# Work moved around and into a gated scan: TensorE's order in the mixer of a two-block network

## What is computed

```
def step(S, inp):
    qc, kc, gc, vc = inp
    b = jnp.cumsum(gc, axis=2)
    diff = b[:, :, :, None, :] - b[:, :, None, :, :]
    decay = jnp.exp(jnp.where(mask, diff, -jnp.inf))
    scores = jnp.einsum("bhtk,bhsk,bhtsk->bhts", qc, kc, decay)
    o = (jnp.einsum("bhts,bhsv->bhtv", scores, vc)
         + jnp.einsum("bhtk,bhkv->bhtv", qc * jnp.exp(b), S))
    b_end = b[:, :, -1, :]
    S = (jnp.exp(b_end)[..., None] * S
         + jnp.einsum("bhsk,bhsv->bhkv", kc * jnp.exp(b_end[:, :, None, :] - b), vc))
    return S, o
...
o = _rmsnorm(o, g_o.reshape(HGRN_HEADS, HGRN_V)).reshape(B, L, B_W).astype(h.dtype)
b_out = o * jax.nn.silu(og)
return jnp.concatenate([a_out, b_out], axis=-1) @ w_out, s_f, s_b
```

## Time and profile before

| | |
|---|---|
| median of 3 runs | 2659.68 us (2659.16 to 2661.69) |
| the profiled execution: its time, its span | 2657.78 us, 2656.0 us |
| mean granted TensorE clock | 0.992 of full |
| PE busy | 2580.4 us, 97% |
| DVE busy | 1200.5 us, 45% |
| ACT busy | 1111.1 us, 42% |
| POOL busy | 889.5 us, 33% |
| HBM | 141 GB/s over the span |

### The profile page before, as it was taken

The page is one execution under the profiler, slowest core; times in us unless marked ns, Lnnn a source line. Parts: engine busy times, 40 slices in busy tenths (PEclk is TensorE's granted clock), DMA queues, the critical chain, the costliest instruction groups (busy, mean ns, idle before and its releaser), DMA issues.

```text
span 2656.0 us, 43966 instructions
## 1 busy us (share of the span) xinstructions
PE 2580.4 (97%) x17121; PEld 2297.4 (86%) x17121; DVE 1200.5 (45%) x1801; ACT 1111.1 (42%) x1544; POOL 889.5 (33%) x1092
## 2 busy tenths in 40 slices
PE   7999999998999999999999999888999999999999
PEld 5777779988887777787777898888999999999999
DVE  4222225237652222252232257654456666556744
ACT  4322334535343222244122247536574554446543
POOL 1222222230022222222233226214554445552554
PEclk9999999999999999999999999999999999999999
DMA  7443542430024334423434434224554444553444
GB/s 278 143 177 139 158 163 98 141 111 1 32 101 162 136 141 152 143 97 142 143 143 143 143 135 151 88 91 152 182 188 163 140 153 181 185 180 112 159 182 151
DMA packets 58527, 376.89 MB, mean 142 GB/s; under 512 B 6223, under 2 KB 12007, under 8 KB 14216
## 3 DMA queue, kind: packets, MB, share of 16 engines
q1 hardware_dynamic: 56988, 371.53, 38.9%
q10 hardware_dynamic: 1388, 3.16, 0.8%
HBM read 370.46 MB, written 3.16 MB: 141 GB/s over the span
## 4 chain that ended last, share of the span: by engine, by line
issue 53%; PE 27%; POOL 17%; DVE 1%; POOLq 0%; DMA 0%; ACT 0%; SPq 0%; DVEq 0%; ACTq 0%
POOL WL L1932 17%; PE PSA L569 8%; PE PSA L570 8%; PE PSA L571 8%; PE PSA L1307 0%; PE PSA L651 0%; POOLq L397 0%; PE PSA L1205 0%; PE PSA L1232 0%; PE PSA L1156 0%; PE PSA L1133 0%; PE PSA L1177 0%; DMA X<-in_x 0%; ACT WH L1374 0%; DMA RAW<-in_weights 0%
## 5 line engine op out<-in xcount | busy, mean ns | idle before, releaser
L1932 POOL TENSOR_TENSOR WL<-RAW,WH 128x256 fp32r<-128x256 f32 x1088 | 889.3, 846 | 1754.0 <-ACT WH L1374 1754.0
L1374 ACT ACTIVATE WH<-RAW 128x1024 fp32r<-128x1024 f32 x544 | 545.8, 1051 | 930.5 <-PE PSA L571 908.8
L1955 DVE TENSOR_TENSOR WL<-RAW,WH 128x1024 fp32r<-128x1024 f32 x272 | 341.8, 1257 | 1100.9 <-ACT WH L1374 1100.6
L569 PE MATMUL PSA<-HH,WH 128*128 128x512 f32 (+1 forms) x1664 | 596.0, 358 | 17.4 <-DVE WL L1955 6.2
L570 PE MATMUL PSA<-HL,WH 128*128 128x512 f32 (+1 forms) x1664 | 588.0, 353 | 0.0
L571 PE MATMUL PSA<-HH,WL 128*128 128x512 f32 (+1 forms) x1664 | 587.4, 353 | 0.0
L569 PE MATMUL PSA<-GH,WH 128*128 128x256 f32 (+1 forms) x1664 | 526.6, 316 | 4.8 <-DVE GL L1972 4.8
L570 PE MATMUL PSA<-GL,WH 128*128 128x256 f32 (+1 forms) x1664 | 521.1, 313 | 0.0
L571 PE MATMUL PSA<-GH,WL 128*128 128x256 f32 (+1 forms) x1664 | 520.9, 313 | 0.0
L569 PEld LDWEIGHTS PSA<-HH,WH 128*128 128x128 f32 x1664 | 315.3, 189 | 77.8 <-issue 25.1
L571 PEld LDWEIGHTS PSA<-HH,WL 128*128 128x128 f32 x1664 | 315.4, 190 | 43.1
(11 more groups left out here) (329 smaller groups left out, 2958.0 us busy)
## 6 DMA issues: line engine op xcount, KB each, us to landing
RAW<-in_weights SPq DMA_DIRECT2D x272, 1024.0 KB, 4.8
ADA<-in_w_ada SPq DMA_DIRECT2D x65, 1024.0 KB, 4.8
Zada<-in_w_ada SPq DMA_DIRECT2D x7, 1024.0 KB, 15.2
scratch_bias<-BREL ACTq DMA_DIRECT2D x1, 2048.0 KB
SUMS<-in_c_sums SPq DMA_DIRECT2D x1, 1664.0 KB, 10.1
TB<-scratch_bias SPq DMA_DIRECT2D x1, 1536.0 KB, 11.0
X<-in_x SPq DMA_DIRECT2D x1, 1024.0 KB, 6.1
X<-in_ctx SPq DMA_DIRECT2D x1, 1024.0 KB, 8.7
```

The costliest lines, as they stand in the source:

```text
L569: pe.matmul(out, a_hi, b_hi, start=start, stop=False)
L1374: act.activation(WH[:, j, 4 * h:4 * h + 4, :], RAW[:, j, 4 * h:4 * h + 4, :], ACT.Copy)\
L1932: ins = pool.tensor_tensor(WL[:, j, kb, :], RAW[:, j, kb, :], WH[:, j, kb, :].bitcast(F32), ALU.subtract)
L1955: dve.tensor_tensor(WL[:, j, 0:4, :], RAW[:, j, 0:4, :], WH[:, j, 0:4, :].bitcast(F32), ALU.subtract)\
```

## The change

It touches PE's order in the mixer, the banks for the turned keys, and one place in ACT's order. In short:

- `chain_decays` moves from behind the second `chain_update` to before the first; ACT takes its exponents before the chain's fourth.
- The keys turn through bank 6 (forward) and bank 5, later 3 (backward). The first three banks of arguments no longer wait for their copies; the fourth does. PE no longer waits for all states before it turns the keys: each bank waits for its own.
- `level_args` is called for two banks at a time: two banks before `scores(g, 0)`, two between that and `scores(g, 1)`.
- `output_sums` stands before the turned keys and arguments of its group, no longer behind its scores.
- The 16 products of the end are cut up (`first_rows`): eight stand ahead of, between and right behind the last scores, output and sums, two more before `DIAG`, six behind it.

```diff
+        def keys_bank(tb, d):
+            return bank(6) if d == 0 else bank(3 if tb else 5)
...
                 def chain_decays():
                     for i, (d, tb, _, enters) in enumerate(CHAIN):
+                        if i >= 3:
+                            n.take(glo_ready)
...
                 read_out(ph)
+                chain_decays()
                 for i in range(len(CHAIN)):
                     chain_update(i)
                     if i + 3 < len(CHAIN):
                         chain_args(i + 3)
-                    if i == 1:
-                        n.take(glo_ready, 2)
-                        chain_decays()
-                n.take(exp_ready, 3)
-                n.take(state_ready, 3)
-                pe.wait_ge(dec_ready, l + 1)
+                n.take(glo_ready, 2)
                 def k_transposed(tb):
-                    if tb:
-                        pe.wait_ge(exp_ready, exps + 16 * tb - 2)
+                    if tb == 0:
+                        n.take(exp_ready, 3)
+                    else:
+                        pe.wait_ge(exp_ready, exps + 16 * tb)
+                    if tb >= 2:
+                        n.take(o_read)
...
-                def level_args(g):
+                def level_args(g, banks):
                     tb, p = g // 4, g % 4
-                    for b in range(4):
+                    for b in banks:
                         d, hh = b // 2, b % 2
-                        if p == 0 and b < 2:
-                            n.take(kf_ready)
-                        elif g:
+                        if g:
                             pe.wait_ge(exp_ready, exps + 4 * (g - 1) + b + 1)
+                        elif b < 3:
+                            n.take(state_ready)
+                        else:
+                            pe.wait_ge(dec_ready, l + 1)
+                        if p == 0 and b == 3:
+                            n.take(kf_ready, 2)
...
                 k_transposed(0)
-                level_args(0)
-                for g in range(groups):
-                    if g + 1 < groups:
-                        if g % 4 == 3:
-                            k_transposed(g // 4 + 1)
-                        level_args(g + 1)
-                    scores(g)
+                level_args(0, range(4))
+                for g in range(last):
+                    if g > 4 and g % 4 == 3:
+                        output_sums(g // 4 - 1)
+                    if g % 4 == 3:
+                        k_transposed(g // 4 + 1)
+                    level_args(g + 1, (0, 1))
+                    scores(g, 0)
+                    level_args(g + 1, (2, 3))
+                    scores(g, 1)
                     if g > 4 and g % 4 == 1:
                         output(g // 4 - 1)
-                    if g > 4 and g % 4 == 3:
-                        output_sums(g // 4 - 1)
-                output(tbs - 1)
-                output_sums(tbs - 1)
+                output_sums(tbs - 2)
                 n.skip(exp_ready, 4 * groups)
                 pe.wait_ge(exp_ready, n.at(exp_ready))
+                for m in range(2):
+                    first_rows(0, 0, m)
+                scores(last, 0)
+                first_rows(0, 1, 0)
+                scores(last, 1)
+                first_rows(0, 1, 1)
+                first_rows(0, 2, 0)
+                output(tbs - 1)
+                first_rows(0, 2, 1)
+                first_rows(0, 3, 0)
+                output_sums(tbs - 1)
                 n.skip(picked, 2 * groups)
...
+                first_rows(0, 3, 1)
+                for m in range(2):
+                    first_rows(1, 0, m)
                 n.take(o_read)
                 for h in range(4):
...
                         .then_inc(pe_to_dve, 1)
+                for kb in range(1, 4):
+                    for m in range(2):
+                        first_rows(1, kb, m)
```

More of the change, by code:

```diff
@@ L954, in chain_args @@
                     d, tb, _, _ = CHAIN[i]
-                    n.take(glo_ready)
-                    if i >= 3:
+                    if i < 3:
+                        n.take(glo_ready)
+                    else:
                         n.take(exp_ready)
@@ L1018, in level_args, with scores @@
                         mm.then_inc(arg_ready, 1)
-                def scores(g):
+                def scores(g, v):
                     tb, p = g // 4, g % 4
[L1022 to L1032, removed]
+                    n.take(lr_ready)
+                    if g:
+                        pe.wait_ge(picked, picks + 2 * (g - 1) + v + 1)
+                    for h in range(4):
+                        out = bank(4 + v)[:, P * h:P * h + P]
+                        if 2 * p + v < LEVELS:
+                            mm = pe.matmul(out, LK[:, g % 2, v, h, :], RQ[:, g % 2, v, h, :], start=True, stop=True)
+                        else:
+                            mm = pe.matmul(out, KS[:, h, :], Q[:, h, P * tb:P * tb + P], start=True, stop=True)
+                    mm.then_inc(score_ready, 1)
                 def output(tb):
-                    if tb:
+                    if tb == tbs - 1:
                         n.take(o_read)
@@ L1051, in output_sums, with first_rows @@
                     mm.then_inc(osum_ready, 1)
+                down = PLAN[PLAN.index(ph) + 2]
+                def first_rows(j, kb, m):
+                    if j == 0:
+                        pe.wait_ge(gl_ready, n.at(gl_ready) + kb + 1)
+                    slot_half(down["slot"] + j, kb)
+                    w = slice(P * m, P * m + P)
+                    three(bank(2 * j + m)[:, 0:P * tbs], WH[:, j, kb, w], WL[:, j, kb, w], GH[:, kb, 0:P * tbs],
+                          GL[:, kb, 0:P * tbs], kb == 0, False)
@@ L1053, in mixer @@
                 groups = 4 * tbs
+                last = groups - 1
                 k_transposed(0)
-                level_args(0)
-                for g in range(groups):
-                    if g + 1 < groups:
-                        if g % 4 == 3:
-                            k_transposed(g // 4 + 1)
-                        level_args(g + 1)
-                    scores(g)
+                level_args(0, range(4))
[8 more added lines that the diff above has]
+                    scores(g, 1)
@@ L1062, in mixer @@
                     if g > 4 and g % 4 == 1:
                         output(g // 4 - 1)
-                    if g > 4 and g % 4 == 3:
-                        output_sums(g // 4 - 1)
-                output(tbs - 1)
-                output_sums(tbs - 1)
+                output_sums(tbs - 2)
                 n.skip(exp_ready, 4 * groups)
                 pe.wait_ge(exp_ready, n.at(exp_ready))
-                n.skip(picked, 2 * groups)
[L1071 to L1080, removed]
+                for m in range(2):
+                    first_rows(0, 0, m)
@@ L1834, in mixer @@
                     chain_exp(i)
-                chain_exp(3)
                 act.wait_ge(dec_mm, l + 1)
@@ L1840, in mixer @@
                 ins.then_inc(dec_ready, 1)
-                for i in range(4, len(CHAIN)):
+                for i in range(3, len(CHAIN)):
                     chain_exp(i)
@@ L1849, in k_copy @@
                     for d in range(2):
-                        act.activation(KK[:, d, tb, :], bank(d), ACT.Copy).then_inc(kf_ready, 1)
+                        act.activation(KK[:, d, tb, :], keys_bank(tb, d), ACT.Copy).then_inc(kf_ready, 1)
                 def level_exps(g):
```

3 lines of the change are left out of this document (2 added, 1 removed).

## The result

The changed kernel takes 2639.8 us (median of 4 runs, 2638.42 to 2642.14), the kernel before 2659.89 us in the same session (2659.16 to 2661.69). The ratio is 0.9924, with a 95% interval of 0.9907 to 0.9942: 20 us faster. The profiled execution took 2638.42 us, with a span of 2636.6 us, 19.4 less than before.

The account below looks back on a forecast made before the run. PE, busy 97% of the span, was taken as the bound. Gains of 11.0 (layer 0) and 13.4 (layer 1), 24.4 us, less 1.7, took 22.7 off 2659.7: 2637.0, stated as 2636.5; range 2628 to 2647 for 8 in 10.

Parts of the forecast that it names:

- layer 0, first four groups: Loop, from DVE's start to the turned keys: 13.9 us in place of 12.3, a loss of 1.6.
- layer 0, later blocks: Loop, three token blocks after the first four groups: each loses 1.2 us against 20.4 before.
- layer 1, loop: Loop of layer 1: 1.6 us lost in the first four groups and 1.2 in one block, 2.8 together.
- Part 1: Chain up to DVE's first group: it starts earlier, 6.5 us gained in layer 0 and 7.0 in layer 1.
- Part 2: The loop: splitting the arguments makes PE wait, 5.2 us lost in layer 0 and 2.8 in layer 1.
- The circle: Loop, arguments to scores and back: 4.8 us against PE's own 3.9, so PE waits 0.9 in two groups of four.
- The wait for copied keys: Loop, PE's wait before arguments (0.7 on average, and the restart): it goes, winning back 0.9 us a block.
- Part 3: End of each layer's mixer: products placed in the waits gain 9.7 us in layer 0 and 9.2 in layer 1.
- Half clock at the ends: Rival at the mixers' ends: half clock stays, keeping 3.5 us in layer 0 and 5 in layer 1; 2644, chance 0.20.
- come into the loop: Rival: the loop falls to half clock, a group taking 7.8 us for 4.8; 2672 with 12 such groups, chance 0.03.
- The reserve: Taken off the whole gain: 1.7 us for one half-clock stretch, of 3.4 us or twice that, at no known place.

Follow-up runs that it names:

- e2: The changed kernel with three banks of arguments ahead of the first scores and one behind them, in place of two and two: 2636.8 us.
- e8: e1 with the decays' two-column matmuls made 128 columns wide, so its decays are other sums than the reference's: 2628.8 us.
- e1: The changed kernel with only the split undone, all four banks of arguments ahead of both scores again: 2631.5 us.
- e3: The kernel before with only the loop's split of the arguments, nothing else moved: 2671.8 us.
- e6: The changed kernel with the turned keys back in banks 0 and 1 and the old waits: 2648.7 us.
- e4: The changed kernel with the decays' two-column matmuls back behind the second update and their exponents behind ACT's fourth step: 2648.0 us.
- e5: The changed kernel with the end of before put back, 16 products in one piece ahead of `DIAG`: 2660.7 us.
- e9: e1 with six unused 512-column matmuls in PE's idle time directly ahead of layer 1's two-column matmuls: 2629.8 us.

## Why the prediction was right

The forecast was 2636.5 us with a range of 2628 to 2647; measured were 2639.8. Step by step, as distances between the starts that it named:

| step | forecast | measured |
|---|---|---|
| layer 0, chain to first group | 6.5 | 22.34 - 17.89 = 4.5 |
| layer 0, first four groups | -1.6 | 12.26 - 14.22 = -2.0 |
| layer 0, later blocks | -3.6 | -1.8, -1.0, -0.3 = -3.1 |
| layer 0, end | 9.7 | 37.0 - 27.1 = 9.9 |
| layer 1, chain to first group | 7.0 | 27.30 - 21.59 = 5.7 |
| layer 1, loop | -2.8 | -2.0 - 1.1 = -3.1 |
| layer 1, end | 9.2 | 29.7 - 21.4 = 8.3 |
| sum | 24.4 | 20.2 |

(At the ends the 1.0 us of two banks of arguments that now stand behind the scores is taken off and put into the loop.)

- **Part 1.** The mechanism was right: no gap ahead of the two-column matmuls, all states written at once behind the updates. The states were out at 619.2, though, and not at 617.5, and the keys turned 4.0 us earlier, not 5 to 6. The size was off by 3.3 us in both layers together, and that was nearly all the clock. The forecast priced all of layer 0's chain at full clock, although the kernel before loses 1.7 us there (4 us at 0.57); the same 4 us stayed. In e2 and e8, without half clock in layer 0's chain, the distance is 16.27, a gain of 6.1 beside the forecast 6.5. In layer 1 the two-column matmuls waited for `Zfm` as foreseen. The forecast let the clock fall 1.5 us behind their start and still gave them 3.5 us, their length at full clock; it fell 1.6 us behind their start (1683.5), and they took 5.3.
- **Part 2.** The circle was 4.89 for the estimated 4.8, the waits 0.98 and 0.83 for the estimated 0.9. They stand in two groups of each four, as forecast; the extra work of the other two fills the wait. The first four groups lost 2.0 for 1.6. e1, e2 and e3 show that it is the split that does this. That the loop's loss came out at 8.2 us for the forecast 8.0 is in part luck. The forecast was 11.6 for the split, 3.6 won back from the keys and nothing for the moved sums, whose work was to fill a wait. By the rows of e3 the split alone costs 10.0, and keys and sums together win back 1.8: two misses of nearly the same size.
- **The wait for copied keys** was put down as 0.9 a block won back. e6 confirms the size with 0.85, and so does layer 1, where no sums were moved, with 0.8 (e3 against the change). What the forecast lacked is the cost of the moved sums, 1.7 us by e6 and e3 with the keys in their old banks. Without the split less of the keys' gain is left: e1 goes through layer 0's three later blocks in 57.7 us, the kernel before in 58.8. The waits of 0.69 for copied keys are gone there, but each block has a wait of 0.66 for right factors where before it had one of 0.2 to 0.3.
- **Part 3.** Right in layer 0. In layer 1 the five small waits (0.28, 0.30, 0.20, 0.46, 0.18) add up to 1.4 of the 1.9 that the forecast had left, yet the gain is 0.9 short. The sum of the work at the matmuls' pace was too small: ahead of each idle time the last matmul's flight (0.28 for 0.12 of pace) isn't covered, some 0.16 five times, and one product starts 0.18 late at 1753.51. That is read from the rows alone; no run varied it, and it leaves some 0.4 of the 1.4 that are missing in the work unexplained.
- **The rivals.** Half clock at the ends didn't stay: 1.00 from 702 to 720, and 1.00 from 1732 to 1775.5. Nor did it come into the loop: 1.00 from 640 to 700, although PE waited 0.8 to 1.0 in every plain group. The kernel that the Trainium skill tells of in the section cited for that rival (TensorE: Matmul & The Clock Gate, "A second HAM failure mode: psum-queue depth-cycling") had its clock swing with short idle times between groups; this trace's loop does not agree, with 1.00. In e4, though, one stretch of 3.5 us at 0.51 stood in the first group (from 628.5), from just behind a wait of 1.76.
- **The reserve** of 1.7 for a stretch that couldn't be placed was of the right kind and too small: the chains came out 3.3 short, nearly all by the clock, and 0.8 went behind layer 1's mixer, where the first sums take 2.08 in the half-clock stretch from 1775.5. Its length of 3.4 is in no row: those last 7 us and lose 3.4; the shorter ones last 3.5 to 4 and lose 1.7.

## What to carry to other kernels

Before splitting a producer's batch to feed two consumers sooner, add up the circle from one release to the next: where it is longer than the work of the engine that is the bound, the split costs that difference each time round, and a run with the split alone shows it at once. At the end of a phase, independent matmuls placed one by one into the waits are worth the waits and, as here, as much again in clock. When comparing versions, look at each run's time times its mean granted clock too: within a kernel it spread by 5 us at most, where the times spread by up to 11. But it also takes out half clock that cost nothing, so the distances between starts in the trace should say the same.

## What the runs showed of the hardware

- The half-clock stretches around the two mixers lasted 3.5 to 4, 7 to 7.5 or 10.5 to 11 us, and once 18 (e5). PE kept issuing in most of them, and the two-column matmuls then started 0.21 us apart in place of 0.11, those of 128 columns too (e8).
- The same code falls to half clock in one kernel and not in the other (layer 0's chain: e1 and e9 for 4 us, e5 for 7.5, e2 and e6 not at all, with the same order up to there), and one kernel's runs differ in mean clock by up to 0.006, and in time by 11 us (e5). What decides it stayed open: neither filling the second of the two idle times nor spreading the narrow matmuls took it away in layer 1.
- Six 512-column matmuls put into an idle time of 1.5 us cost nothing (e9 against e1), and gained nothing either.
